# The opening of a long kernel: x sent first, the first root made wide, the rotary angles moved to the end of the opening

## What is computed

```python
c_act = jax.nn.silu(c)
mod = c_act @ w_ada[l] + b_ada[l]
sh1, sc1, gt1, sh2, sc2, gt2 = jnp.split(mod, 6)
h = rms_norm(x, norm1[l]) * (1.0 + sc1) + sh1
proj = h @ w_in[l]
q, k, v, g, u, vs, p, gate_cols = split_columns(proj)
y_ret = retention(q, k, v, g, positions)      # q, k turned by rotary(...)

def rms_norm(x, gain):
    return x * lax.rsqrt(jnp.mean(x * x, axis=-1, keepdims=True) + 1e-6) * gain

def rotary(x, positions):
    ang = positions[:, :, None] * inv_freq       # 64 frequencies
    cos, sin = jnp.cos(ang), jnp.sin(ang)
    x1, x2 = halves of x
    return concatenate([x1 * cos - x2 * sin, x2 * cos + x1 * sin])
```

## Time and profile before

| | us |
|---|---|
| median of 3 runs | 3226.9 |
| lowest and highest | 3226.77, 3227.86 |
| span of the profiled execution (its first to its last instruction) | 3225.6 |
| TensorE busy in the span | 3207.7 (99%) |
| VectorE, ScalarE, GpSimd busy | 1898.1, 1158.9, 239.3 |

### The profile page before, as it was taken

The page is one execution under the profiler, slowest core; times in us unless marked ns, Lnnn a source line. Parts: engine busy times, 40 slices in busy tenths (PEclk is TensorE's granted clock), DMA queues, the critical chain, the costliest instruction groups (busy, mean ns, idle before and its releaser), DMA issues.

```text
span 3225.6 us, 43771 instructions
## 1 busy us (share of the span) xinstructions
PE 3207.7 (99%) x15424; PEld 2655.3 (82%) x15424; DVE 1898.1 (59%) x2745; ACT 1158.9 (36%) x1533; POOL 239.3 (7%) x249
## 2 busy tenths in 40 slices
PE   8999999999999999999999999999999999999998
PEld 7788888888888788888888888768888888878887
DVE  8455567564447455667564445666665744586656
ACT  4433333332223433243332223354333523553423
POOL 2100000100001100000100002051000101320001
PEclk9999999999999999999999999999999999999999
DMA  7146325422222156424422222203322322122222
GB/s 259 66 159 207 129 93 168 142 95 96 98 98 92 60 162 201 139 87 164 146 98 98 97 93 94 79 27 98 104 96 94 109 95 94 49 79 98 98 98 78
DMA packets 100059, 357.84 MB, mean 111 GB/s; under 512 B 11328, under 2 KB 13648, under 8 KB 99808
## 3 DMA queue, kind: packets, MB, share of 16 engines
q1 hardware_dynamic: 99248, 353.99, 32.9%
q0 software_dynamic: 688, 2.21, 0.2%
HBM read 354.06 MB, written 2.10 MB: 110 GB/s over the span
## 4 chain that ended last, share of the span: by engine, by line
PE 98%; DVE 1%; ACT 0%; DMA 0%; DVEq 0%; issue 0%; ACTq 0%; POOL 0%; POOLq 0%; SPq 0%
PE pb L622 25%; PE pb L623 25%; PE pb L624 25%; PE pb L654 2%; PE pb L655 2%; PE pb L658 2%; PE pb L702 2%; PE pb L701 2%; PE pb L700 2%; PE pb L1024 1%; PE pb L1400 1%; PE pb L1401 1%; PE pb L1402 1%; PE pb L931 1%; PE pb L1014 1%; PE pb L932 1%
## 5 line engine op out<-in xcount | busy, mean ns | idle before, releaser
L1472 ACT ACTIVATE hi<-raw 128x1024 fp32r<-128x1024 f32 x548 | 575.8, 1056 | 979.2 <-PE pb L624 678.0
L2013 DVE TENSOR_TENSOR lo<-raw,hi 128x1024 fp32r<-128x1024 f32 x548 | 667.7, 1223 | 356.1 <-ACT hi L1472 310.8
L622 PE MATMUL pb<-yH,hi 128*128 128x512 f32 (+1 forms) x1664 | 644.8, 388 | 0.0
L624 PE MATMUL pb<-yH,lo 128*128 128x512 f32 (+1 forms) x1664 | 644.6, 387 | 0.0
L623 PE MATMUL pb<-yL,hi 128*128 128x512 f32 (+1 forms) x1664 | 644.6, 387 | 0.0
L622 PE MATMUL pb<-hH,hi 128*128 128x512 f32 x1512 | 590.6, 391 | 0.0
L623 PE MATMUL pb<-hL,hi 128*128 128x512 f32 x1512 | 589.0, 390 | 0.0
L624 PE MATMUL pb<-hH,lo 128*128 128x512 f32 x1512 | 588.9, 389 | 0.0
L622 PEld LDWEIGHTS pb<-yH,hi 128*128 128x128 f32 x1664 | 312.7, 188 | 63.6
L623 PEld LDWEIGHTS pb<-yL,hi 128*128 128x128 f32 x1664 | 312.7, 188 | 63.5
L624 PEld LDWEIGHTS pb<-yH,lo 128*128 128x128 f32 x1664 | 312.7, 188 | 63.1
(11 more groups left out here) (433 smaller groups left out, 4041.2 us busy)
## 6 DMA issues: line engine op xcount, KB each, us to landing
raw<-stream SPq DMA_DIRECT2D x648, 512.0 KB, 3.3
yF<-first SPq DMA_DIRECT2D x8, 512.0 KB, 13.0
act<-first SPq DMA_DIRECT2D x8, 512.0 KB, 15.9
x<-xT SPq DMA_DIRECT2D x4, 512.0 KB, 7.8
outT<-act SPq DMA_DIRECT2D x7, 256.0 KB, 2.2
tab<-decay SPq DMA_DIRECT2D x1, 1024.0 KB, 6.4
scr<-ws POOLq DMA_DIRECT2D x2, 256.0 KB, 3.0
scr<-bs POOLq DMA_DIRECT2D x2, 256.0 KB, 3.4
```

The costliest lines, as they stand in the source:

```text
L622: pe.matmul(out, whi, ahi, start=first, stop=False)
L624: return pe.matmul(out, wlo, ahi, start=False, stop=last)
L1472: act.activation(hi[:, s], raw[:, s], ACT.Copy).then_inc(hi_ready, 1)
L2013: dve.tensor_tensor(lo[:, s, 0:width], raw[:, s, 0:width], hi[:, s, 0:width].bitcast(F32), ALU.subtract).then_inc(lo_ready, 1)
```

## The change

It touches the opening alone.

- SyncE issues x first. c, the positions, the identity and the small constants go out on ScalarE's queue, before ScalarE's first activation. `v2` is issued by GpSimd only after its seven rests `hL`, and VectorE waits for it where it is first used, late in the second layer.
- The positions are one row of 512. VectorE makes them f32, and TensorE spreads them over the partitions with one multiply (`spread_pos`). Ahead of it stand 14 filler multiplies on a cleared patch (`warm_up`).
- The first norm: TensorE multiplies the squares with a matrix that is -1/2048 everywhere, 512 columns wide, in five accumulating multiplies (k=0, k=1, and three pair sums). ScalarE takes the reciprocal root of minus twice that, and its square; VectorE adds one Newton step in two instructions. The column sums, the five small steps and the spread of the root go.
- The angles: c1 is taken off early; c2, c3 and the clamp after VectorE's last `hL`. Absolute value, sine and cosine stand on ScalarE behind its last `hH`.

```diff
-            sp.dma_start(cs[:, 0], cvec).then_inc(c_in, 16)
-            sp.dma_start(scr[:, 0:S].bitcast(I32), pos).then_inc(pos_in, 16)
-            sp.dma_start(cst[:, C_EDGE:C_ALL], consts[:, C_EDGE:C_ALL]).then_inc(freq_in, 16)
-            sp.dma_start(cst[:, 0:C_FOLD], consts[:, 0:C_FOLD]).then_inc(setup_in, 16)
             for n in range(4):
                 sp.dma_start(x[:, 2 * n:2 * n + 2], xT[:, 2 * n:2 * n + 2]).then_inc(x_in[n], 16)
...
             pool.dma_start(v1[:], vec1).then_inc(vec1_in, 16)
-            pool.dma_start(v2[:], vec2).then_inc(vec_in, 16)
...
+            pool.dma_start(v2[:], vec2).then_inc(vec_in, 16)
             for l in range(LAYERS):
...
+            def warm_up():
+                pe.wait_ge(fill_ready, 1)
+                for _ in range(14):
+                    pe.matmul(pb[:, 1, 0:P], st[:, 0, 0:P], st[:, 0, 0:P], start=True, stop=True)
+            def spread_pos():
+                pe.wait_ge(freq_in, 16)
+                pe.wait_ge(pos_row, 1)
+                pe.matmul(pb[:, 2], one_row.to_broadcast([1, P]), scr[0:1, S:2 * S], start=True, stop=True
+                          ).then_inc(pos_spread, 1)
             def first_norm():
-                keep_busy(15, 1)
-                pe.wait_ge(half_squares, 1)
-                column_sums(0, True, False)
-                keep_busy(6, 1)
-                pe.wait_ge(half_squares, 2)
-                column_sums(4, False, True).then_inc(summed, 1)
+                for k in (0, 1):
+                    pe.wait_ge(squared, k + 1)
+                    pe.matmul(pb[:, 4], mean_col.to_broadcast([P, P]), A[:, k], start=k == 0, stop=False)
+                for n, k in enumerate((2, 4, 6)):
+                    pe.wait_ge(pair_squares, n + 1)
+                    ins = pe.matmul(pb[:, 4], mean_col.to_broadcast([P, P]), A[:, k], start=False, stop=k == 6)
+                ins.then_inc(summed, 1)
                 squares.next(KT)
-                keep_busy(6, 1)
-                spread_rows()
-                keep_busy(2, 1)
+                keep_busy(8, 1)
                 shift_column(0)
-                keep_busy(3, 1)
+                keep_busy(8, 1)
...
+            warm_up()
+            spread_pos()
             pe.wait_ge(setup_in, 16)
...
+            act.dma_start(cs[:, 0], cvec).then_inc(c_in, 16)
+            act.dma_start(scr[0:1, 0:S].bitcast(I32), pos).then_inc(pos_in, 16)
+            act.dma_start(cst[:, 0:C_FOLD], consts[:, 0:C_FOLD]).then_inc(setup_in, 16)
+            act.dma_start(cst[:, C_EDGE:C_ALL], consts[:, C_EDGE:C_ALL]).then_inc(freq_in, 16)
...
-            act.activation(cs[:, 2, 0:1], epsc, ACT.Sqrt)
-            act.wait_ge(trig_arg, 1)
-            act.activation(cosT, sinT, ACT.Abs)
-            root()
+            act.activation(cs[:, 2, 0:1], epsc, ACT.Abs_reciprocal_sqrt)
+            act.wait_ge(summed, sums.next())
+            act.activation(first_root, pb[:, 4], ACT.Abs_reciprocal_sqrt, bias=epsc, scale=-2.0)
+            act.drain()
+            act.activation(first_rows, first_root, ACT.Square).then_inc(rooted, 1)
...
-                elif k == RING - 1:
-                    act.activation(sinT, sinT, ACT.Sin).then_inc(trig, 1)
-                    act.activation(cosT, cosT, ACT.Sin, scale=-1.0, bias=cst[:, C_HALFPI:C_HALFPI + 1]
-                                   ).then_inc(trig, 1)
+            act.wait_ge(trig_arg, 1)
+            act.activation(cosT, sinT, ACT.Abs)
+            act.drain()
+            act.activation(sinT, sinT, ACT.Sin).then_inc(trig, 1)
+            act.activation(cosT, cosT, ACT.Sin, scale=-1.0, bias=cst[:, C_HALFPI:C_HALFPI + 1]
+                           ).then_inc(trig, 1)
...
             first_sum(0)
-            rstd()
             first_sum(1)
             dve.drain().then_inc(mod_ready, 1)
-            dve.wait_ge(rs_full, rf.next())
+            dve.wait_ge(rooted, roots.next())
+            dve.scalar_tensor_tensor(first_rows, pb[:, 4], -0.5 * EPS, first_rows, ALU.add, ALU.mult)
+            dve.drain()
+            dve.scalar_tensor_tensor(pb[:, 5], first_rows, 1.5, first_root, ALU.add, ALU.mult)
+            dve.drain()
...
+            for c in (c2, c3):
+                whole_turns_off(c)
+            dve.tensor_scalar(sinT, sinT, 3.1415925, -3.1415925, ALU.min, ALU.max)
+            dve.drain().then_inc(trig_arg, 1)
+            dve.sem_inc(layer_done, 1)
```

More of the change, by code:

```diff
@@ L48 @@
 C_SLOPE = C_FREQ + 4
-C_ALL = C_SLOPE + 24
+C_MEAN = C_SLOPE + 24
+C_ALL = C_MEAN + 1
 V_N1, V_N2, V_ADA, V_GAIN, V_BP, V_PS, V_ALL = 0, 8, 16, 64, 72, 80, 88
@@ L153, in build @@
         epsc = cst[:, C_EPS:C_EPS + 1]
+        mean_col, one_row = cst[:, C_MEAN:C_MEAN + 1], cst[0:1, C_SIGN:C_SIGN + 1]
+        first_root, first_rows = tab[:, 0:S], tab[:, S:2 * S]
         Mf = act3[:, 2 * KT:3 * KT].rearrange("p k s -> p (k s)")
@@ L293, in build @@
         pos_in = sem("pos_in")
+        pos_row = sem("pos_row")
+        pos_spread = sem("pos_spread")
+        fill_ready = sem("fill_ready")
         vec_in = sem("vec_in")
@@ L710, in keep_busy @@
                     pe.matmul(pb[:, bank, 0:P], ident, ones, start=True, stop=True)
[L712 to L717, removed]
             def shift_column(i):
@@ L1606, in late_tiles @@
                     work(n)
-            spreads = Count(4 * LAYERS - 1)
+            spreads = Count(4 * LAYERS - 2)
             def late_rows(double=False):
@@ L2239, in _, with square_pair, whole_turns_off @@
             turns_i, turns = scr[:, 0:S].bitcast(I32), scr[:, S:2 * S]
-            dve.tensor_copy(turns, turns_i)
-            dve.drain()
-            dve.tensor_scalar(sinT, turns, cst[:, C_FREQ:C_FREQ + 1], None, ALU.mult)
+            def square_pair(n):
+                dve.wait_ge(squared, n + 2)
+                dve.tensor_tensor(A[:, n], A[:, n], A[:, n + 1], ALU.add)
+                dve.drain().then_inc(pair_squares, 1)
+            def whole_turns_off(c):
+                dve.scalar_tensor_tensor(sinT, turns, -c, sinT, ALU.mult, ALU.add)
+                dve.drain()
+            dve.wait_ge(pos_in, 16)
+            dve.tensor_copy(turns[0:1], turns_i[0:1])
+            dve.drain().then_inc(pos_row, 1)
+            dve.wait_ge(freq_in, 16)
+            dve.wait_ge(pos_spread, 1)
+            dve.tensor_scalar(sinT, pb[:, 2], cst[:, C_FREQ:C_FREQ + 1], None, ALU.mult)
             dve.drain()
@@ L2245, in _ @@
             dve.drain()
+            square_pair(2)
             dve.tensor_copy(turns, turns_i)
             dve.drain()
-            for c in (c1, c2, c3):
-                dve.scalar_tensor_tensor(sinT, turns, -c, sinT, ALU.mult, ALU.add)
-                dve.drain()
-            dve.tensor_scalar(sinT, sinT, 3.1415925, -3.1415925, ALU.min, ALU.max)
-            dve.drain().then_inc(trig_arg, 1)
-            dve.sem_inc(layer_done, 1)
-            def square_pair(a, b, count):
-                dve.wait_ge(squared, count)
-                dve.tensor_tensor(A[:, a], A[:, a], A[:, b], ALU.add)
-                dve.drain()
-            square_pair(0, 1, 2)
-            square_pair(2, 3, 4)
-            square_pair(0, 2, 4)
-            dve.sem_inc(half_squares, 1)
-            square_pair(4, 5, 6)
-            square_pair(6, 7, 8)
-            square_pair(4, 6, 8)
-            dve.sem_inc(half_squares, 1)
+            square_pair(4)
+            whole_turns_off(c1)
+            square_pair(6)
             gain, bias = v1[:, V_N1:V_N1 + 8], v1[:, V_ADA:V_ADA + 16]
@@ L2888, in constants @@
     c[:, C_HALFPI] = np.pi / 2
+    c[:, C_MEAN] = -0.5 / D
     c[:, C_SLOPE:C_SLOPE + 24] = np.exp2(-8.0 * np.arange(1, 25) / 24)
@@ L2983 @@
         "cvec": columns(a["c"][0]),
-        "pos": np.ascontiguousarray(np.broadcast_to(a["positions"], (P, S))),
+        "pos": np.ascontiguousarray(a["positions"].reshape(1, S)),
         "consts": c, "decay": decay, "tables": tables, "vec1": vec1,
```

13 lines of the change are left out of this document (3 added, 10 removed).

## The result

| | before | after |
|---|---|---|
| median, 8 runs each | 3227.5 | 3236.6 |
| lowest and highest | 3226.77, 3228.34 | 3234.31, 3237.4 |
| span of the profiled execution | 3225.6 | 3232.6 |
| x times root starts | 20.30 | 22.09 |
| second tiles start | 48.80 | 54.12 |

The ratio of after to before is 1.0027, 95% interval [1.0019, 1.0035]. The prediction said 3228.2 (3225.5 to 3231.5): it is wrong, above its range. The eight spans run from 3232.6 to 3235.7, and the time outside the span is 1.7 or 1.8 in each, so what varies lies inside the span.

What follows compares the result with a forecast made beforehand. TensorE, busy 3207.7 of 3225.6 us, was taken as the bound, so only its waits matter: 3226.9, minus 2.9 for the earlier x times root, plus 4.2 for the late angles, gives 3228.2 us (range 3225.5 to 3231.5).

Steps and rivals of the forecast that it cites:

- x first: Opening transfers: x issued 1.9 us earlier plus 1.1 from less traffic, last x landing at 10.1, squares ending at 11.3.
- Filler: TensorE's opening: 14 filler multiplies from about 1.1 take 5.1 us and end at 6.2.
- Landing of the frequencies: Opening: frequencies, issued fourth on ScalarE's queue, land at 7.0, as v2 took 4.8 us; positions' product waits for them.
- the upper bound: Latest landing of the frequencies in the opening, 10.1, if the engines finish x first.
- First norm: Opening: positions, spread of c, five wide sums to 14.4, root 2.9 us; x times root starts 2.9 earlier than 20.30.
- the 17.4: Forecast start of x times root at the end of the first norm, against 20.30 before.
- the late-vector rival: Opening: frequencies land behind x at 10.1, 3.1 later, 3231.3; 11%, a third of it with lower clock near 3235.
- Middle: VectorE's eight rounds after x times root: unchanged, so the 2.9 us gain goes through to 45.04.
- Angles late: Between first and second tiles: late angles delay ScalarE's hi copy, leaving TensorE idle 4.1 to 4.2 us.
- Clock behind the stall: Rival: idle stretch before second tiles lowers TensorE's clock, 1.8 us more, 3230.0; chance 15%.

Runs made afterwards that it cites:

- e6: Changed kernel with the frequencies issued ahead of the identity on ScalarE's queue, third instead of fourth: 3235.47 us.
- e1: Changed kernel with the angles' last steps (c2, c3, clamp, Abs, Sins) taken back into the opening: 3231.38 us.
- e4: Kernel before with only the late angles: c2, c3, clamp behind VectorE's last hL, Abs and Sins behind ScalarE's last hH: 3234.11 us.
- e5: Changed kernel with the first of VectorE's two Newton instructions written to PSUM instead of SBUF: 3236.74 us.
- e12: Changed kernel with the first Newton step in PSUM and 17 fillers ahead of the second tiles, none added at the opening: 3233.92 us.
- e9: Changed kernel with the first Newton step in PSUM, 32 fillers instead of 14 at the opening and 17 ahead of the second tiles: 3232.01 us.
- e10: Changed kernel with small vectors ahead of x on SyncE's queue, first Newton step in PSUM, all VectorE angle steps before the pair sums, Abs and Sins early: 3226.59 us.
- e7: Changed kernel with small vectors ahead of x on SyncE's queue, angles' last steps back in the opening, first Newton step in PSUM: 3229.78 us.
- e2: Changed kernel with c, positions, frequencies and identity issued on SyncE's queue ahead of x: 3231.56 us.
- e11: As e10, but x first, ScalarE's queue ordered positions, frequencies, c, identity, and spread of c behind the second wide sum: 3227.0 us.
- e8: Changed kernel with ScalarE's queue reordered (positions, frequencies, c, identity), spread of c before the fourth wide sum, angles early, Newton step in PSUM: 3230.78 us.
- e3: Changed kernel with 32 instead of 14 fillers at the opening and 17 more ahead of the second tiles: 3234.05 us.

## Why the prediction was wrong, point by point

Two steps failed: the landing of the frequencies, taken as 7.0 and measured as 10.1, and the clock, taken at its full level throughout, which fell in the idle stretch that the late landing made and again behind the late angles. The 8.4 us between 3228.2 and 3236.6 are made up so: x times root 4.7 later than forecast (3.1 the landing, 1.8 the slower product and spread, less 0.2), the middle and the stall together 0.7 shorter, slow multiplies behind the stall 1.7, what the other executions of after lose beyond the profiled one 2.1, and 0.6 because before's median is 3227.5 with eight runs and was 3226.9 with three.

- **x first: right.** Last x forecast at 10.1, read at 9.8; squares forecast to end at 11.3, their last row ends at 11.0. It bought nothing, since nothing waited for them.
- **Filler: right.** Forecast to end at 6.2; TensorE goes idle at 5.9. That is the short end: in the nine other profiles with the same 14 fillers they end between 6.3 and 7.2.
- **Landing of the frequencies: the step that failed.** "The nearest row is v2, which travelled on another queue beside x and took 4.8 us. I take that: 7.0." They landed at 10.1. That is the number of the upper bound, by luck: the bound supposed that x is served first, and e6 rules that out. v2 is 212 KB from GpSimd's queue, sent when the other queue held small pieces too. Here 46.5 KB stood last of four transfers of 434 packets, beside 4 KB packets of x, and e6 shows that the place in the own queue decides. The Trainium skill (DMA: Bandwidth & Descriptors, Queues, rings and completion order) says that an engine takes a packet from each queue in turn. e6 agrees with it; I drew the wrong sum from it. By the estimate under e6 each small row waits for 4 KB of x, so many small rows are slow. It covers the step between places, not the whole: c, first in its queue, took 2.9 us more than alone, and 8 turns are 1.3. What the rest is stays open. The step cost 3.1 us.
- **First norm: the chain right, its clock wrong.** Five wide sums and the root measured 4.50 and 2.96 against 4.6 and 3.0. But the product took 1.29 instead of 0.9 and the spread of c 3.24 instead of 1.9, at the lower level behind 4.2 us of idleness. With 3.1 + 0.4 + 1.4 - 0.2 the 17.4 become 22.1. This is the late-vector rival with the lower clock in both places, which the text had at 3234.9 and a third of 11%.
- **Middle: right within 0.4.** The rounds are alike; a gap of 0.59 us before k=2 of the kernel before is gone.
- **Angles late: right.** Forecast 4.1 to 4.2; last hH to second tiles 3.95 more, and e1 and e4 confirm the place.
- **Clock behind the stall: given 15%, came true.** "Here 4.2, and no row shows such a gap" was no ground for 1.00. Priced at 1.8, read at 1.71 in the profile, 2.5 to 2.8 in the median (e5 to e12).
- **Nothing late left out?** The long Newton step wasn't foreseen, but it isn't part of after's loss: 0.70 in the profile, and e5 gained nothing.

The median once more: of the 9.1, the lowered clock is about 4.5 (e5 to e9: 4.7, or 4.4 after the difference in before). What is left in e9 is 4.5 above before: x times root at 21.34 instead of 20.30, 1.0, and 3.5 of late angles. The profiled execution had a milder clock than e5's (0.50 in three stretches of 1 us against five). That the other timed runs of after differ from it by the clock alone isn't traced run by run; their mean granted clock reads 0.997 against its 0.998, and the range narrows from 3.1 to 1.1 with the fillers.

## What to carry to other kernels

Whoever sends the big transfer first must still ask which small one the next engine waits for: a small transfer that starts a chain belongs ahead of the big one on the same queue, or first on its own. An idle stretch that a reordering makes can cost twice, once as the wait and again as slow multiplies behind it; the second only where TensorE sets the pace. Before moving work off an engine, see whether it fits into that engine's own idle time: the angles' last steps cost nothing ahead of the pair sums (e10), about 3 us behind the tile sums (e7 against e10, the held-up clamp included) and 5 to 6 at the end.

## What the runs showed of the hardware

- **VectorE and GpSimd shut each other out.** With two operands in SBUF, VectorE's 0.70 us instruction took 2.64 and 2.69 when GpSimd's copy had started first; when VectorE was first by 0.23 (after), GpSimd's copy took 2.69 instead of 2.35. With one operand in PSUM neither suffered (e9). The clamp, one SBUF input, took 2.41 and 2.56 instead of 0.43. The Trainium skill (SBUF — State Buffer, Who interferes with whom) says that whoever starts first holds a shared pair of ports for its whole instruction, against two SBUF inputs and against VectorE's two-port modes; both kinds agree with these rows. That the clamp runs in such a mode is not shown here.
- **Small transfers beside a large one.** 4 KB took 4.5 us (after) instead of 1.6 (e2); 46.5 KB took 7.8, 6.5 or 5.2 as the fourth, third or second of its queue (after, e6, e11) instead of 1.9 (e2).
- **The granted clock falls behind some idle stretches and not behind others, and their length doesn't decide it.** At the turn to the second tiles TensorE was idle 3.8 us and the next stretches read 0.50 to 0.78 (after, e2, e4, e5, e6). In the opening it fell to 0.66 behind 4.21 us (after), to about 0.50 behind 3.71, 3.08, 2.86 and 1.76 (e12, e1, e5, e6), and to 0.66 behind 0.87 and 0.95 (e8, e11). Ahead of the first tiles it read 0.66 behind 4.01 (e7) and 0.71 behind 3.20 (e8). It stayed at 1.00 behind 2.00 in e10's opening, and ahead of the first tiles behind 1.79 (e1) and 1.77 (e3). What tells these apart stays open.
- **A lower clock costs only where TensorE sets the pace.** e11 had 0.66 in 10 to 15 and e10 had 1.00, and x times root starts at 20.13 in both; e7 had 0.66 in 25 to 30 and no later second tiles for it.
